# One stage for the odd layer's mixing and its output product, with the softmax exchange issued by SyncE

## The reference, cut to what matters

```
def dilated_group_attention(q, k, v, window, dilation, slopes): ...   # banded attention at dilation 1, 4 and 16
...
h  = rmsnorm_2(x, odd_norm_2)
q, k, v, gate_c, b, c, xx, gate_d = split(h @ odd_w_in_2)             # width 3*3*1024 + 1024 + 4*1024
c_part = joint softmax over the three dilations of attention(q, k, v), times silu(gate_c)     # 8 slots of 128
d_part = short_conv(c * xx, odd_conv_w_2) times b and silu(gate_d)                            # 1024 channels
x   = x + concat(c_part, d_part) @ odd_w_out_2                        # K = 2048, N = 1024
out = rmsnorm_2(x, final_norm_2)
```

## Time and profile before

| | |
|---|---|
| median of three runs | 3559.72 us |
| the profiled execution, its own time | 3552.2 us |
| its span, first to last instruction | 3550.5 us |
| mean granted TensorE clock | 0.954 of full |
| PE busy | 3218.1 us, 91% |
| DVE, ACT, POOL busy | 47%, 34%, 42% |
| DMA queue q1 (SP) | 300076 packets, 309.13 MB |
| DMA queue q10 (ACT) | 63462 packets, 21.43 MB |
| odd layer's preparation and conv pairs | about 1955 to 2348 us from the start |
| heads' pairs | about 2348 to 3297 us |
| end of the last head, barrier, first y tiles | 3297 to 3350 us |
| output product | 3350 to 3527 us |
| last norm and store | 3527 to 3551 us |

### The profile page before, as it was taken

The page is one execution under the profiler, slowest core; times in us unless marked ns, Lnnn a source line. Parts: engine busy times, 40 slices in busy tenths (PEclk is TensorE's granted clock), DMA queues, the critical chain, the costliest instruction groups (busy, mean ns, idle before and its releaser), DMA issues. The chain is left out here.

```text
span 3550.5 us, 43411 instructions
## 1 busy us (share of the span) xinstructions
PE 3218.1 (91%) x16176; PEld 2627.9 (74%) x16176; DVE 1685.8 (47%) x2414; ACT 1193.5 (34%) x2010; POOL 1475.8 (42%) x909
## 2 busy tenths in 40 slices
PE   5988996877799799999999699999999999999698
PEld 3667885764688567778877588887788778778587
DVE  4665233835799543311112755555455455445412
ACT  4255223713577421001110322234334334343301
POOL 2330331042222123343333788865555555555142
PEclk8989998988899899999999799999999999999799
DMA  8121113073799811321113122222221221221421
GB/s 289 33 84 37 42 30 99 20 238 106 279 397 398 300 53 48 107 80 41 43 30 124 51 78 63 69 54 46 45 51 46 40 52 53 44 40 42 137 89 66
DMA packets 368331, 349.80 MB, mean 99 GB/s; under 512 B 85398, under 2 KB 337098, under 8 KB 361874
## 3 DMA queue, kind: packets, MB, share of 16 engines
q1 hardware_dynamic: 300076, 309.13, 26.6%
q10 hardware_dynamic: 63462, 21.43, 2.8%
q0 software_dynamic: 4608, 16.78, 1.8%
HBM read 291.25 MB, written 52.63 MB: 97 GB/s over the span
## 5 line engine op out<-in xcount | busy, mean ns | idle before, releaser
L273 POOL TENSOR_TENSOR w_hi<-w_raw,zero_col 128x1024 fp32r<-128x1024 f32 x87 | 166.1, 1909 | 841.1 <-PE mls_z L308 204.5
L3026 POOL TENSOR_TENSOR odd_quarter_lo<-odd_w_sums,odd_quarter_hi 128x512 fp32r<-128x512 f32 x224 | 301.4, 1348 | 248.3 <-ACT odd_quarter_hi L3021 247.5
L3063 PE MATMUL first_z<-odd_t_hi,odd_quarter_hi 128*128 128x512 f32 x784 | 329.0, 420 | 31.5 <-DVE odd_t_lo L3578 25.2
L3063 PE MATMUL odd_z<-odd_t_hi,odd_quarter_hi 128*128 128x512 f32 x784 | 326.4, 416 | 8.0 <-POOL odd_quarter_lo L3026 6.6
L3026 POOL TENSOR_TENSOR odd_quarter_lo<-odd_raw,odd_quarter_hi 128x512 fp32r<-128x512 f32 x168 | 235.5, 1402 | 211.7 <-ACT odd_quarter_hi L3021 207.9
L3065 PE MATMUL first_z<-odd_t_hi,odd_quarter_lo 128*128 128x512 f32 x784 | 309.9, 395 | 0.0
L3064 PE MATMUL first_z<-odd_t_lo,odd_quarter_hi 128*128 128x512 f32 x784 | 309.0, 394 | 0.0
L3065 PE MATMUL odd_z<-odd_t_hi,odd_quarter_lo 128*128 128x512 f32 x784 | 307.8, 393 | 0.0
L3064 PE MATMUL odd_z<-odd_t_lo,odd_quarter_hi 128*128 128x512 f32 x784 | 306.7, 391 | 0.0
L3021 ACT CAST odd_quarter_hi<-odd_w_sums 128x512 fp32r<-128x512 f32 x224 | 139.2, 622 | 313.8 <-PE odd_z L3065 152.5
L276 POOL TENSOR_TENSOR w_lo<-w_raw,w_hi 128x1024 fp32r<-128x1024 f32 x87 | 233.3, 2681 | 6.8
(11 more groups left out here) (576 smaller groups left out, 7646.5 us busy)
## 6 DMA issues: line engine op xcount, KB each, us to landing
odd_raw<-in_odd_w_in SPq DMA_DIRECT2D x224, 256.0 KB, 3.3
raw_gate<-in_w_gate SPq DMA_DIRECT2D x16, 2048.0 KB, 15.7
raw_up<-in_w_up SPq DMA_DIRECT2D x16, 2048.0 KB, 14.8
raw_down<-in_w_down SPq DMA_DIRECT2D x16, 2048.0 KB, 14.5
w_raw<-in_even_w_in SPq DMA_DIRECT2D x40, 512.0 KB, 5.3
start_w_mod<-in_w_mod SPq DMA_DIRECT2D x11, 1024.0 KB, 10.8
w_raw<-in_w_in SPq DMA_DIRECT2D x16, 512.0 KB, 6.0
scan_w_mod<-in_w_mod SPq DMA_DIRECT2D x8, 1024.0 KB, 11.2
```

The source lines that it names most:

```text
L273: pool.tensor_tensor(w_hi[:, u], w_raw[:, u], zero_col[:, 0:1].to_broadcast([P, KT * P]).rearrange("p (k n) -> p k n", k=KT), ALU.add).the ...
L3026: pool.tensor_tensor(self.w_lo[:, n % self.SLOTS], self.source(m, i), self.w_hi[:, n % self.SLOTS].bitcast(F32), ALU.subtract).then_inc(se ...
L3063: pe.matmul(to, self.w_hi[:, slot, kt], t_hi[:, kt], start=(kt == 0), stop=False)
```

## The change: what it does

There is one stage now; `phase_last`, its barrier and its loads are gone. What is otherwise:

1. **Start.** DVE scales all four quarters of x first and then forms the four token sums and all seven lo parts; before, POOL made two of the seven (`token_parts`), and scaling and sums were mixed.
2. **Y.** After each result ACT makes y's hi part and DVE its lo part at once (`split_y`, `lo_of_y`), and SP stores both (`store_y`), 1 MB a tile where ACT stored 0.5 MB.
3. **Exchange.** For heads 0 to 6 SP issues the stores, the loads and the waits between them, in the middle of its queue of weight loads. The shares of a head are made in the next head's first pair. For the last head ACT still issues.
4. **Sums and scores.** The head's sums begin after product 3 of the next head's first pair (before: product 2) and end in product 2 of the second pair (before: 1); the first eight scores come in products 3 to 6 of the second pair (before: 2 to 5). DVE's `take_p` and `bias` move accordingly.
5. **Output product.** Its 16 units follow the last pair in the same block. Y tiles 0 to 14 are loaded back as hi and lo once the token tiles are used up, from product 1 of the last pair on. The last head's sums stand between the matmuls of units 0 and 1, and the last y isn't stored at all. x comes by one DMA of 4 MB.

```diff
 @block.sync
-for m in range(PAIRS):
-    quarters.load(sp, m, ...)
-sp.wait_ge(quarters.product, 7 * PAIRS)
-pre.load(sp)
...
+for h in range(C_SLOTS):
+    m = DIL_AT + HEAD_PAIRS * h
+    load(m + 2)
+    if h:
+        store_y(KT + h - 1, (dil_hi, dil_lo))
+    load(m + 3)
+    load(m + 4)
+    if h == C_SLOTS - 1:
+        break
+    store_lse(sp, h)            # waits lse_done, 7 stores of single floats
+    load(m + 5)
+    load_joint(sp, h)           # waits lse_stored
+    load(m + 6, (0,))           # the first three quarters
+    store_share(sp, h)          # waits share_done
+    load_share(sp, h)           # waits share_stored, 7 loads
+    load(m + 6, (1,))           # the fourth quarter
...
+load_unit(0)
+sp.wait_ge(y_stored, 32 * (KO - 1))
+for kt in range(4):
+    load_y(kt, quarters.product, 7 * (PAIRS - 1) + 2 + kt // 2)
+load_unit(1)
+for kt in range(4, 12):
+    load_y(kt, quarters.product, 7 * (PAIRS - 1) + 2 + kt // 2)
...
 @block.tensor
 for i in range(7):
-    multiply(m, i, {... sum_pair(h - 1, 2 * (i - 3) + kt // 2) for kt in (1, 3)} if h and i >= 3 else None)
+    multiply(m, i, {... sum_pair(h - 1, 2 * (i - 4) + kt // 2) for kt in (1, 3)} if h and i >= 4 else None)
     if h and i == 0:
         turn_v(h - 1, 2)
-    if h and i == 2:
+    if h and i == 3:
         begin_sums(h - 1)
...
+h = C_SLOTS - 1
+for k in range(2 * KT):
+    pe.wait_ge(wo_split, k + 1)
...
+    for kt in range(KT):
...
+        if k == 0 and kt == 0:
+            turn_v(h, 2)
+        if k == 0 and kt == 2:
+            begin_sums(h)
+        if k < 2 and 3 <= KT * k + kt < 3 + NU // 2:
+            sum_pair(h, KT * k + kt - 3)
...
 @block.vector      (first and second pair of a head)
     if h:
         rows(h - 1, 2)
-        factor(h - 1)
+        share_out(h - 1)
     u2(m)
     u3(m)
     if h:
-        take_p(h - 1, 0, 6)
+        factor(h - 1)
     c21(m)
...
     c12(m)
     if h:
-        take_p(h - 1, 18, NU)
+        take_p(h - 1, 14, 18)
     u2(m + 1)
     if h:
+        take_p(h - 1, 18, 22)
+    u3(m + 1)
+    if h:
+        take_p(h - 1, 22, NU)
         gate_sum(h - 1)
-    bias(h, 0)
-    u3(m + 1)
-    bias(h, 1, 2)
     c21(m + 1)
-    bias(h, 3, 4)
+    bias(h, 0, 1)
     c22_u4(m + 1)
-    bias(h, 5, 6)
+    bias(h, 2)
+    if h:
+        lo_of_y(KT + h - 1, silu, dil_hi, dil_lo)
+    bias(h, 3)
```

More of the change, by code:

```diff
@@ new lines, in _ @@
+                    for k in range(4, 2 * KT):
+                        load_unit(k)
+                    for j in range(BLOCKS):
+                        for half in range(2):
+                            sp.wait_ge(last_rows_out[half], j + 1)
+                        sp.dma_start(out[0][j * P:(j + 1) * P, :], row_tiles[:, j % SETS, :]).then_inc(rows_stored[j % SETS], 16)
+                    for u in range(SETS):
+                        sp.wait_ge(rows_stored[u], 16 * len(range(u, BLOCKS, SETS)))
@@ L3399, in _ @@
                                 turn_v(h, 1)
+                    z = [first_z, second_z]
                     h = C_SLOTS - 1
-                    turn_v(h, 2)
-                    begin_sums(h)
-                    for s in range(NU // 2):
-                        sum_pair(h, s)
+                    for k in range(2 * KT):
+                        n, first = unit(k)
+                        u = k % 2
+                        pe.wait_ge(wo_split, k + 1)
+                        if k < 2:
+                            pe.wait_ge(quarters.evicted, 7 * (PAIRS - 1) + (5, 7)[k])
+                        elif n >= 2 and first == 0:
+                            pe.wait_ge(z_free, n - 1)
+                        if k == 2:
+                            pe.wait_ge(y_loaded[4], 32 * (KO - 1 - KT))
+                        for kt in range(KT):
+                            c = first + kt
+                            if k == 0:
+                                pe.wait_ge(y_loaded[c // 2], 64)
+                            if c == KO - 1 and n == 0:
+                                pe.wait_ge(y_lo_done, KO)
+                            for w, rhs, begin, end in ((wo_hi, y_parts[c][0], c == 0, False), (wo_hi, y_parts[c][1], False, False), (wo_lo, y_parts[c][0], False, c == KO - 1)):
+                                for b in range(2):
+                                    ins = pe.matmul(z[n % 2][:, b, :], w[:, u, kt], rhs[:, b * HALF:(b + 1) * HALF], start=begin, stop=end)
+                            if kt == KT - 1:
+                                ins.then_inc(projected, 1)
+                            if k == 0 and kt == 0:
[4 more added lines that the diff above has]
+                                sum_pair(h, KT * k + kt - 3)
@@ L3887, in add_up @@
+                    lo_of_y(KO - 1, silu, *y_parts[KO - 1])
                     def add_up(n):
```

524 lines of the change are left out of this document (271 added, 253 removed).

## The result

The changed kernel took 3618.01 us (median of four runs, 3615.16 to 3623.79), the kernel before 3558.74 us in the runs beside it: a ratio of 1.017, with a 95% interval of 1.015 to 1.019. It is 59 us slower; 37 were forecast, and the time lies in the stated range.

What follows compares the result with a forecast made beforehand. TensorE was taken as the bound, with only its idle time to win. Terms -5 + 0 + 53 - 11 = +37 us on 3552.2 gave 3589, or 3597 on the runs' median; range 3526 to 3640.

Steps and rivals of the forecast that it cites:

- Start: Before the convolution: lo parts made by DVE alone let PE begin product 1 sooner; 2.5 to 7 us won, 5 taken.
- The convolution's 0: Convolution pairs: ACT's cast and DVE's subtract for y stay hidden beside PE, DVE busy 186 of 335 us; 0 taken.
- First wait: Start of each head: weight quarters queued behind SP's log-sum-exp stores make PE wait 4.5 us, against 1.7 before; bounds 0 and 6.
- turn_v's 3.0: Heads: PE's 3.0 us wait a head for DVE's last join ahead of `turn_v` goes.
- Shares: At `begin_sums`: shares made after the next head's `turn_v` and copies; PE waits 2.9 us a head, against 0.6; bounds 0 and 5.
- Copies: Second pair, `sum_pair` 9 and 11: needed copies stand behind joins on DVE; 1.6 us twice, 3.2 a head.
- Scores: Scores 4 and 5 in product 5: banks wait for product 4's joins and `lo_of_y`; 2.3 us a head, nothing before.
- Sum of the waits in the heads: Heads: 12.9 us a head against 5.3, 7.6 more, times 7 is 53 us; bounds -20 to +96.
- the likeliest case: Rival A, whole kernel: waits as forecast, 3597 us, its own range 3573 to 3622; chance 0.47.
- the worst case: Rival D, heads: quarters only after stores, 16.4 us a head, clock falling to 1.2 GHz for another 10; 3643 us; chance 0.15.
- Tail: After the last pair: last exchange delayed to 3325 by y loads, end at 3516 against 3527; gain 11 us.
- my bound of 25: Last head's exchange, sharing DMA engines with 15.7 MB of y: between 0 and 25 us later, the middle taken.

## Why the prediction was right, and where its terms were off

The forecast was slower by 37 us, by waits of 4.5, 2.9, 3.2 and 2.3 us a head. Step by step:

- **Start, -5**: right, -5.1 at the second product, -6.1 at the end of the convolution. The convolution's 0 is within that. The terms are averages that hide two sizes: 19.63 us for four are 6.5, 6.6, 3.4 and 3.4, and after the change three of the six still take 3.4 beside POOL, so all seven are there 4.0 us sooner and not 4.9.
- **First wait, 4.5 a head**: measured 4.7, with two errors that cancel. POOL's first sum was put at E + 0.6 and came at E - 0.2 (E: the end of the head's last product, 3220.77), but then POOL has three sums and a lo part to do and not two and one, 5.3 us and not 3.9. The rates of the earlier trace rows were a good base although they were taken from two queues, since the quarters come as late from either. The reason that the prediction leaned on, "weights behind the stores in SP's queue", is right in time and wrong in kind: a request in another ring, made as late, waited as long.
- **turn_v's 3.0 gone**: right for the heads. In the tail it came back: 11.9 us for the last joins, which stand on DVE behind the joint's steps. It costs nothing there, because the shares come later still.
- **Shares, 2.9**: measured 2.8, partly by luck. The share went out 8.1 us behind the head's start and not 5.7, but PE came to `begin_sums` some 2 us later than I had counted as well, behind a stretch at half clock. And what I took for the time of an exchange is mostly a place in DVE's order, as the swap of two lines shows.
- **Copies, 3.2**: 2.8, in fifteen waits of 1.3 us each and not fourteen of 1.6.
- **Scores, 2.3**: 0.7. I let the second score wait for `lo_of_y` and two joins in full; it was mis-sized by a factor of three.
- **Sum of the waits in the heads**: 12.9 against 5.3 a head were forecast, +53 us; measured 77.8 against 38.1, +39.7. The step that failed is the one that held the clock at the old level in the likeliest case: the same matmuls were busy 21.4 us longer, some 15 of them by the clock. I had given the clock 10 us, and only in the worst case. Two errors of opposite sign, 13 us too much wait and 21 us too little busy time, leave +61.5 for +53; that the heads' figure comes so near is luck.
- **Tail, -11**: measured +2.8. The mechanism was right (one wait at `begin_sums`, of 22.1 us, behind another of 11.9), the term mis-sized: the exchange took 31 us longer and not 12, more than my bound of 25. I had priced the delay by the bytes of y as a whole, but loads of y lie beside each transfer of the exchange, and each got longer: the stores took 24.9 us instead of 16.6, from the joint's load to the exponential it was 10.8 instead of 3.3, from the share's store to the first share load 8.0 instead of 1.7, the seven loads were 10.9 us being issued instead of 3.8, and from the last of them to the scaling it was 7.3 instead of 1.9. With tiles 4 to 14 held back the tail is 15 us shorter.

Of the span's 62.6 us, 4.4 lie ahead of the odd layer, in code that the change doesn't touch and whose length varies by 10 us between profiles; why it varies stays open.

## What to carry to other kernels

A wait on TensorE may cost twice, once as a wait and once as slower matmuls behind it; read the second part from the busy time of the same instructions in both kernels, since no wait shows it. It doesn't come back with each wait that goes: here it stayed when the first wait went, and was gone when the last of them was down to 1.4 us. Before small-element stores start, have the next loads already asked for; a second queue didn't help here. And when a result goes through DRAM and back, look first at where its last arithmetic stands in an engine's order: here two lines swapped on DVE were worth about as much as moving the loads ahead of the stores.

## What the runs showed of the hardware

- Stores of single floats (3072 of them, in seven DMAs) take 16 to 19 us in a head from the first issue to the load that waits for them, and fill the DMA engines: share 0.96 to 1.03 at 24 to 45 GB/s with the reads in the same ring, 0.80 to 0.84 at 37 to 88 GB/s with three of the four reads in ACT's; the quarters came equally late. The same data in rows of 32 bytes took 1.5 us from issue to landing.
- Beside large loads, issuing is slow as well: ACT took 10.9 us to issue seven loads of shares while the DMA engines moved y at a share of 1.05 (3385.57 to 3396.47), and 3.8 with y held back, at 0.29; in a head SP takes 3.8 for the same seven, with only weights around them.
- The clock over heads 0 to 6: 0.97 with waits of 4.7, 2.8 and twice 1.3 us a head, the same with the first taken away and the second grown to 4.0; 0.99 with the 4.0 alone; 1.00 with 1.4 alone or none. The time at half clock in the eight heads and PE's busy time went with it: 58 and 71 us with 982 and 984, 24 with 960, none with 949 and 948.
- Subtractions of 128x2048 on DVE took 2.3 us without POOL beside them, 6.5 beside one of the same size on POOL (itself 4.7 to 5.3), and 3.4 beside POOL's of 128x512, which took 3.3 themselves and 1.3 elsewhere.
